# Decoder trunk: the MLP's weight sums go from VectorE to GpSimd, and the last group's squares, residual tiles and square sums are handed to other engines

## The reference, cut to what matters

```python
x = x + mixer_out(attn, rec, lp)              # MLA heads + RG-LRU
x = x + mem_attend(rmsnorm(x, norm_mem_g), mem_k, mem_v, lp)
h = rmsnorm(x, norm_mlp_g)
x = x + jnp.square(jax.nn.relu(h @ w_up)) @ w_down     # w_up 1024x4096, w_down 4096x1024
y = rmsnorm(x, final_norm_g)
```

## Time and profile before

| | before |
|---|---|
| median of 3 runs | 1017.05 us (1015.78 to 1017.05) |
| the profiled execution | 1017.48 us, its span 1015.3 us |
| PE busy | 973.6 us, 96% of the span |
| VectorE, GpSimd, ScalarE busy | 675.1, 430.2, 383.1 us |
| granted TensorE clock, mean | 0.989 |
| chain that ended last | PE 74%, VectorE 14%, ScalarE 4%, GpSimd 3% |

### The profile page before, as it was taken

The page is one execution under the profiler, slowest core; times in us unless marked ns, Lnnn a source line. Parts: engine busy times, 40 slices in busy tenths (PEclk is TensorE's granted clock), DMA queues, the critical chain, the costliest instruction groups (busy, mean ns, idle before and its releaser), DMA issues.

```text
span 1015.3 us, 20122 instructions
## 1 busy us (share of the span) xinstructions
PE 973.6 (96%) x8319; PEld 876.8 (86%) x8319; DVE 675.1 (66%) x1051; ACT 383.1 (38%) x774; POOL 430.2 (42%) x284
## 2 busy tenths in 40 slices
PE   6999999999999999999999999889999999999987
PEld 6989898766677777999975799889999999999986
DVE  5789978378655555564155366779577856957686
ACT  7334265465444443121045222334234333424344
POOL 4545579601011112555320155845375466628340
PEclk8999999999999999999999999999999999999999
DMA  8323355524277772832193036223340514144012
GB/s 235 81 67 83 104 158 141 152 95 186 116 277 272 282 279 69 280 96 85 30 398 138 1 90 180 64 83 93 95 125 23 166 43 125 43 125 114 12 42 88
DMA packets 140560, 130.41 MB, mean 128 GB/s; under 512 B 13477, under 2 KB 133170, under 8 KB 136630
## 3 DMA queue, kind: packets, MB, share of 16 engines
q1 hardware_dynamic: 134888, 88.55, 29.0%
q0 software_dynamic: 2304, 37.75, 9.6%
q10 hardware_dynamic: 3278, 2.83, 0.8%
HBM read 123.53 MB, written 5.03 MB: 127 GB/s over the span
## 4 chain that ended last, share of the span: by engine, by line
PE 74%; DVE 14%; ACT 4%; issue 3%; POOL 3%; DMA 2%; SPq 0%; DVEq 0%; ACTq 0%; POOLq 0%
PE gps L655 33%; PE gps L1286 7%; PE aux L1286 7%; PE gps L1015 5%; PE aux L1029 3%; PE aux L1056 3%; PE gps L791 2%; PE gps L1171 1%; PE gps L1253 1%; PE aux L1035 1%; POOL wlo L580 1%; PE gps L1091 1%; DVE pw_lo L2350 1%; PE aux L967 1%; DVE act_lo L1887 1%
## 5 line engine op out<-in xcount | busy, mean ns | idle before, releaser
L556 POOL TENSOR_SCALAR whi<-wraw 128x1024 fp32r<-128x1024 f32 (+1 forms) x77 | 83.4, 1083 | 291.1 <-PE gps L655 224.9
L655 PE MATMUL gps<-h_hi,whi 128*128 128x272 f32 x640 | 185.7, 290 | 2.6 <-POOL wlo L559 2.6
L655 PE MATMUL gps<-h_hi,wlo 128*128 128x272 f32 x640 | 185.5, 290 | 0.0
L655 PE MATMUL gps<-h_lo,whi 128*128 128x272 f32 x640 | 185.0, 289 | 0.0
L559 POOL TENSOR_TENSOR wlo<-wraw,whi 128x1024 fp32r<-128x1024 f32 (+1 forms) x77 | 178.9, 2323 | 6.4
L655 PE MATMUL gps<-act_hi,whi 128*128 128x272 f32 x448 | 132.5, 296 | 4.8 <-DVE act_lo L1887 4.1
L655 PE MATMUL gps<-act_lo,whi 128*128 128x272 f32 x448 | 130.9, 292 | 0.0
L655 PE MATMUL gps<-act_hi,wlo 128*128 128x272 f32 x448 | 130.4, 291 | 0.0
L592 POOL TENSOR_TENSOR pw_lo<-praw,pw_hi 128x512 fp32r<-128x512 f32 x64 | 94.9, 1491 | 77.7 <-ACT pw_hi L1772 76.9
L655 PEld LDWEIGHTS gps<-h_hi,whi 128*128 128x128 f32 x640 | 120.9, 189 | 3.4 <-POOL wlo L559 3.0
L655 PEld LDWEIGHTS gps<-h_lo,whi 128*128 128x128 f32 x640 | 120.7, 189 | 0.0
(11 more groups left out here) (431 smaller groups left out, 2371.4 us busy)
## 6 DMA issues: line engine op xcount, KB each, us to landing
wraw<-in_w_up_dram SPq DMA_DIRECT2D x32, 512.0 KB, 4.2
praw<-in_w_down_dram SPq DMA_DIRECT2D x32, 512.0 KB, 4.9
wraw<-in_w_in_dram SPq DMA_DIRECT2D x14, 512.0 KB, 4.1
kv<-in_cache_mem_k_dram SPq DMA_DIRECT2D x7, 1024.0 KB, 6.9
kv<-in_cache_mem_v_dram SPq DMA_DIRECT2D x7, 1024.0 KB, 14.0
wraw<-in_w_mem_k_dram SPq DMA_DIRECT2D x16, 256.0 KB, 3.1
wraw<-in_w_mem_v_dram SPq DMA_DIRECT2D x16, 256.0 KB, 3.3
wraw<-in_w_out_dram SPq DMA_DIRECT2D x8, 512.0 KB, 4.9
```

Of the source, the lines that this page charges most:

```text
L556: nc.gpsimd.tensor_scalar(whi[:, slot, 0:n], wraw[:, slot, 0:n], 1.0, 1.0, ALU.mult, ALU.mult).then_inc(pool_step, 1)
L655: mm = nc.tensor.matmul(out_of(a), w_of(w, k), x_of(x, k, part), start=(k == 0 and s == 0), stop=(k == k_tiles - 1 and s == 2))
```

## The change

All sixteen pairs' four sums move from VectorE to GpSimd. GpSimd's work for a pair in the down part is now eight operations in this order: sum 0, sum 1, low 0, low 2, sum 2, low 3, sum 3, low 5. Sum 0 of pair q waits, as before, until all of VectorE's low parts of the pairs before are made (`pair_lo_d`, 3q), since `s_sum` has one buffer.

In the up part GpSimd does the same for pair 4g behind the splits of tiles 2 to 6, and VectorE's low parts 1 and 4 of pair 4g stand behind tiles 2 and 4. Low part 6 of pair 4g is no longer in the up part: `down_pair` now begins with `pair_low(q, 6)` for the first pair of a group too, where it did so only `if p`.

In the last group GpSimd adds up the squares of tiles 1 to 5 (`gather_last`), ScalarE does the high part and the square of two tiles between the casts 2, 3 and 4 of a pair (`final_high`), and PE sums `acc` inside product 6 of the last pair and the squares of tiles 6 and 7 apart, into bank 3 of `gps`.

```diff
 POOL, up part and behind it
-                    for i in {2: (0,), 3: (2, 3), 5: (5,)}[j] if j in (2, 3, 5) else ():
-                        pair_low(4 * g, i)
+                    if j == 2:
+                        pair_sum_of(4 * g, 0)
+                        pair_sum_of(4 * g, 1)
...
                     if (g and j == 1) or (g == GROUPS - 1 and j == 7):
                         for q in range(4 * (g - (j == 1)) + 1, 4 * (g - (j == 1)) + 4):
-                            for i in POOL_LOW:
-                                pair_low(q, i)
+                            pair_sum_of(q, 0)
+                            pair_sum_of(q, 1)
+                            pair_low(q, 0)
+                            pair_low(q, 2)
+                            pair_sum_of(q, 2)
+                            pair_low(q, 3)
+                            pair_sum_of(q, 3)
+                            if q > 13:
+                                gather_last(2 * (q - 14))
+                            pair_low(q, 5)
+                            if q > 13:
+                                gather_last(2 * (q - 14) + 1)
 DVE, down part
-                if p:
-                    pair_low(q, 6)
+                pair_low(q, 6)
                 dve.wait_ge(pair_ps, 7 * q + 2)
                 V.tensor_tensor(x22, x22, c, ALU.subtract).then_inc(pair_ev, 1)
-                if ahead:
-                    pair_sums(q + 1, 0)
-                    pair_sums(q + 1, 1)
...
-                if last and p:
-                    gather_square(3, 2 * p - 2)
-                    gather_square(3, 2 * p - 1)
-                if ahead:
-                    pair_sums(q + 1, 2)
 DVE, up part
-                    if j == 0:
-                        pair_sums(4 * g, 0)
-                        pair_sums(4 * g, 1)
-                    if j == 1:
+                    if j == 2:
                         pair_low(4 * g, 1)
-                        pair_sums(4 * g, 2)
-                    if j == 2:
-                        pair_sums(4 * g, 3)
+                    if j == 4:
                         pair_low(4 * g, 4)
-                    if j == 3:
-                        pair_low(4 * g, 6)
 PE, product 6 of the last pair
+                    if (q, i, k) == (15, 6, 1):
+                        pe.wait_ge(pair_ev, 7 * 15)
+                        pe.wait_ge(nx_acc, 19)
+                        token_sums(acc[:, :], True)
```

More of the change, by code:

```diff
@@ L339, in low_ready @@
             return pair_lo_d, 3 * q + DVE_LOW.index(i) + 1
-        Y_BANKS = (((aux, 0), (aux, 1)), ((gps, 2), (aux, 2)), ((gps, 0), (gps, 3)), ((gps, 1), (aux, 0)),
+        Y_BANKS = (((aux, 0), (aux, 1)), ((gps, 2), (aux, 2)), ((gps, 0), (aux, 3)), ((gps, 1), (aux, 0)),
                    ((gps, 2), (aux, 1)))
@@ L593, in pair_low, with pair_sum_of, gather_last @@
                                         ).then_inc(pair_lo_p, 1)
+            def pair_sum_of(q, n):
+                raw = praw[q % 2]
+                if n == 0:
+                    pool.wait_ge(pair_raw[q % 2], REST_0 + 32 * (q // 2 + 1))
+                    if q:
+                        pool.wait_ge(pair_lo_d, 3 * q)
+                    nc.gpsimd.tensor_tensor(s_sum[:, :], raw[:, 1, 0, :], raw[:, 1, 1, :], ALU.add
+                                            ).then_inc(pair_sum, 1)
+                elif n == 1:
+                    pool.wait_ge(pair_sum, 4 * q + 1)
+                    nc.gpsimd.tensor_tensor(raw[:, 1, 0, :], raw[:, 0, 0, :], raw[:, 1, 0, :], ALU.add
+                                            ).then_inc(pair_sum, 1)
+                elif n == 2:
+                    pool.wait_ge(pair_sum, 4 * q + 2)
+                    pool.wait_ge(pair_lo_p, HALF_0 + 4 * q + 1)
+                    nc.gpsimd.tensor_tensor(raw[:, 0, 0, :], s_sum[:, :], raw[:, 0, 0, :], ALU.add
+                                            ).then_inc(pair_sum, 1)
+                else:
+                    pool.wait_ge(pair_sum, 4 * q + 3)
+                    pool.wait_ge(pair_lo_p, HALF_0 + 4 * q + 3)
+                    nc.gpsimd.tensor_tensor(raw[:, 0, 1, :], raw[:, 0, 0, :], raw[:, 0, 1, :], ALU.add
+                                            ).then_inc(pair_sum, 1)
+            def gather_last(k):
+                if k < 1:
+                    return
+                pool.wait_ge(nx_sq, 5 + 16 + k + 1)
+                if k >= 2:
+                    pool.wait_ge(nx_acc, 14 + k - 1)
+                nc.gpsimd.tensor_tensor(acc[:, :], acc[:, :], sqb[1][:, k % 2, :], ALU.add).then_inc(nx_acc, 1)
             for u in range(U_MLP + 8 * GROUPS):
@@ L630, in _ @@
                     g, j = divmod(u - U_MLP, 8)
-                    for i in {2: (0,), 3: (2, 3), 5: (5,)}[j] if j in (2, 3, 5) else ():
-                        pair_low(4 * g, i)
+                    if j == 2:
+                        pair_sum_of(4 * g, 0)
+                        pair_sum_of(4 * g, 1)
+                    if j == 3:
+                        pair_low(4 * g, 0)
+                        pair_low(4 * g, 2)
+                    if j == 4:
+                        pair_sum_of(4 * g, 2)
+                        pair_low(4 * g, 3)
+                    if j == 5:
+                        pair_sum_of(4 * g, 3)
+                    if j == 6:
+                        pair_low(4 * g, 5)
                     if (g and j == 1) or (g == GROUPS - 1 and j == 7):
                         for q in range(4 * (g - (j == 1)) + 1, 4 * (g - (j == 1)) + 4):
-                            for i in POOL_LOW:
-                                pair_low(q, i)
+                            pair_sum_of(q, 0)
[10 more added lines that the diff above has]
+                                gather_last(2 * (q - 14) + 1)
+                    if g == GROUPS - 1 and j == 7:
+                        gather_last(4)
+                        gather_last(5)
                 if u == U_OUT + 3:
@@ L1264, in moving, with token_sums @@
                         4: r[:, k, 0:HALF], 5: r[:, k, 2 * HALF:3 * HALF], 6: x[:, 4 + k, high]}[i]
+            def token_sums(squares, start):
+                for i in range(5):
+                    n = 128 if i < 4 else TS
+                    mm = nc.tensor.matmul(gps[0:n, 3, i:i + 1], squares[:, 128 * i:128 * i + n], ones[:, 0:1],
+                                          start=(start and i == 0), stop=True, skip_group_check=True)
+                return mm
             def pair_part(q, i, ks):
@@ L1343, in _ @@
             pe.wait_ge(pair_ev, 7 * 15 + 5)
-            for i, z in Y_ORDER[:3]:
+            for i, z in Y_ORDER[:2]:
                 y_turn(i, z)
[L1346 to L1350, removed]
-            pe.wait_ge(nx_sq, 5 + 8 * 3)
[L1352 to L1356, removed]
+            pe.wait_ge(nx_sq, 5 + 8 * 3 - 1)
+            token_sums(sqb[1][:, 0, :], False)
+            pe.wait_ge(nx_sq, 5 + 8 * 3)
+            token_sums(sqb[1][:, 1, :], False).then_inc(nx_ps, 1)
             pe.wait_ge(pair_ev, 7 * 16)
-            for i, z in Y_ORDER[3:]:
+            for i, z in Y_ORDER[2:]:
                 y_turn(i, z)
@@ L1814, in final_high @@
                 act.wait_ge(res_ok, 16 + k + 1)
-                if k < KD - 1:
-                    raw_hi(XG[:, k, :], k, "final_norm_g")
+                raw_hi(XG[:, k, :], k, "final_norm_g")
                 square_of(3, k)
-                if k == KD - 1:
-                    raw_hi(XG[:, k, :], k, "final_norm_g")
-            HIGH_AFTER = {0: (0, 1, 2, 3), 2: (4, 5, 6)}
+            HIGH_AFTER = {1: (0, 1, 2, 3), 3: (4, 5), 5: (6,)}
             for g in range(GROUPS):
@@ L1833, in _ @@
                         pair_copy(pair)
-                    if p < PAIRS - 1:
-                        for i in (0, 1, 2):
+                    for i in range(7):
+                        if p < PAIRS - 1:
                             pair_high(pair + 1, i)
[L1837 to L1844, removed]
+                        if g == GROUPS - 1 and p and i in (2, 4):
+                            final_high(2 * p - 2 + (i == 4))
+            for k in (6, 7):
+                act.wait_ge(res_ok, 16 + k + 1)
+                square_of(3, k)
+            for k in (6, 7):
+                raw_hi(XG[:, k, :], k, "final_norm_g")
             act.wait_ge(nx_var, 7)
@@ L2326, in _ @@
             raw_norm(2, T_MO, "norm_mlp_g")
[L2327 to L2345, removed]
             def pair_low(q, i):
@@ L2418, in down_pair @@
                 V.tensor_tensor(x12, b, x12, ALU.add).then_inc(pair_ev, 1)
-                if ahead:
-                    pair_sums(q + 1, 3)
                 dve.wait_ge(pair_ps, 7 * q + 6)
@@ L2437, in _ @@
                     up_tile(8 * g + j)
-                    if j == 0:
-                        pair_sums(4 * g, 0)
-                        pair_sums(4 * g, 1)
-                    if j == 1:
+                    if j == 2:
                         pair_low(4 * g, 1)
-                        pair_sums(4 * g, 2)
-                    if j == 2:
```

(9 more changed lines are left out.)

## The result

The changed kernel takes 1067.91 us (median of 4 runs, 1067.58 to 1068.95) against 1017.05 (4 runs, 1015.78 to 1019.18) for the kernel before: a ratio of 1.050, 95% interval 1.048 to 1.052. Its profiled execution has a span of 1065.8 us, 50.5 longer, and a mean granted clock of 0.969. The prediction was +49.7.

What follows compares the result with a forecast made beforehand. PE was taken to set the pace, so only 14.9 us could be won; losses of 56.1 (groups 0 to 2), 6.6 (group 3) and 1.9 (up part), less 14.9, gave +49.7: 1067.2 us, range 1055.5 to 1081.

Steps and rivals of the forecast that it cites:

- Part 2: Second pair of groups 0 to 2: late low part 6 delays SP's loads, so PE waits 14.3 us in each.
- Part 1: Down part: GpSimd's eight operations take 11.75 us a pair against PE's 10.55, so PE must wait 1.2 a pair.
- The two meetings of a pair: GpSimd operations beside two of VectorE's three low parts in a pair: 0.44 us extra each.
- rival C: GpSimd, all pairs: nearly every operation meets VectorE and pays 0.44 us, 31 more in all, 1098 us; chance 10%.
- The rule of the Trainium skill: GpSimd and two-input VectorE operations lock shared SBUF ports: up to 0.68 us an encounter, some 5 us over 12 pairs.
- The waits at product 3: Down pairs: PE waits for `p1s` at product 3, 2.0 us in the first pair behind a hold, 1.2 in each following.
- the cover: Products 0 to 2 after a hold: slower matmuls eat into product 3's 2.0 us wait, costing nothing; uncovered, 5 us.
- Group 3: Last group, no holds: waits at product 3 of 2.0, 1.2, 2.0, plus 0.3 and 1.1 in pair 15; 6.6 us together.
- The 14.9 us won: Whole MLP and behind it: 13.1 us of PE's waits and 1.8 of slow clock all go.
- split weights in group 0: First up part: GpSimd's splits and pair operations, 6.1 us against PE's 6.05, have no lead; 1.9 us lost.
- A: Rival: the next group's two tile loads come in time, only the pair rate remains, 1024.3 us; chance 5%.
- B: Rival, not slower: VectorE's low part 6 is done early, loads leave as before, 1015.4 us; chance 3%.

Runs made afterwards that it cites:

- the kernel with the loads first: Changed kernel, but SP issues the next group's two tile loads ahead of pair 4g+2's loads: 1028.9 us, ratio 1.011.
- the kernel without holds: Changed kernel with SP's loads of the next group's tiles issued first and low part 6 of pair 4g made one tile earlier: 1018.39 us, ratio 1.0018.

## Why the prediction held, step by step

- **Part 2, the holds (3 x 14.3 forecast).** Measured 13.8, 14.1 and 14.0: the place, the number of groups and each link of the chain are as forecast. Putting the loads first removes it, and the earlier low part 6 shortens it by its own shift; the move alone makes it in the kernel before.
- **Part 1, the pace (11.75 us a pair forecast).** GpSimd's sum 0 of two pairs that follow each other in group 2 starts at 913.24 and 924.86, 11.6 apart; a pair later, in group 0, it is 11.76 (706.39 and 718.15). On PE, product 3 of the last two pairs comes 11.76 to 11.79 apart in groups 0 to 2. Sum 0 to the end of low part 0 was to take 4.3 us and took 4.4. The operations by themselves, in the columns of the earlier trace rows:

```profile
L592 POOL TENSOR_TENSOR pw_lo<-praw,pw_hi x64: 1262/1292/2057, 643.7 to 1044.0; 128x512 fp32r<-128x512 f32 x64
...
L2388 DVE TENSOR_TENSOR pw_lo<-praw,pw_hi x32: 677/1106/1773, 661.9 to 1043.4; 128x512 fp32r<-128x512 f32 x32
...
L606 POOL TENSOR_TENSOR praw<-praw x16: 1266/1290/1300, 634.4 to 1034.3; 128x512 f32<-128x512 f32 x16
...
L616 POOL TENSOR_TENSOR praw<-praw x16: 1286/1548/1567, 656.3 to 1041.2; 128x512 f32<-128x512 f32 x16
```

  An add on GpSimd costs the 1.29 that was taken from a low part, and the median low part fell from 1.488 to 1.292, since VectorE's sums were what it met (1.492 again in the kernel whose sums went back to VectorE). The two meetings of a pair, taken at 0.44 each, cost 0.45 (low part 0, 1.72 to 1.76 us in the second to fourth pair of a group) and 0.26 (sum 3, the last line). The dear GpSimd of rival C would have needed 1.7. The rule of the Trainium skill that the prediction worked out beside Part 1 ("SBUF — State Buffer", the section "SBUF: two separate sides") was taken there at up to 0.68 an encounter, a pair up to 0.5 longer. The pairs show none of that; the last section has what the rule gives when it is read with the order in which the two begin.
- **The waits at product 3 (18.4 us forecast, 8.5 measured).** The size is off and the sum is not. Where nothing covers them, in the kernel with the loads first, they are 15.0: the list counts from the end of the product before, and product 3 comes 1.84 and 1.15 us late there where 2.0 and 1.2 were forecast (the prediction's own S + 10.95 less S + 8.85 is 2.1). The other 6.5 us are the cover. After each hold PE's granted clock is 0.50, the 1.2 GHz level; here the one in group 1:

```profile
805.00:809.00 4.00, 0.56 (x2) 0.59 (x3) 3.01 (x6) 1.75 (x3) 3.92 (x4) 0.50 0.00 0
809.00:813.00 4.00, 4.00 (x20) 4.00 (x19) 1.95 (x4) 1.14 (x2) 3.86 (x4) 0.50 0.00 0
```

  PE is slow where it would otherwise have waited for `p1s`, and GpSimd's pace sets the end of the group either way. What had been taken from the 3.7 us wait, 1.8 us, was too small for a hold of 14: in groups 1 and 2 products 0 to 2 took 7.3 us instead of 4.5, and the loss of 2.8 also ate the wait of the pair that followed. The cover, 2.0 + 1.2 + 1.2 = 4.4 a group in the forecast, held: from the start of the pair behind the hold to product 3 of the group's last pair it is 29.90, 29.91 and 29.90 us in the three groups, and 29.9 in the kernel with the loads first, where no clock was lost there.
- **Group 3.** Product 3 waits 1.64, 0.97 and 1.64 in the three pairs (2.0, 1.2, 2.0 forecast), 0.17 for low part 0 of pair 15 (0.3) and 1.23 for `acc` (1.1).
- **The 14.9 us won.** The waits of the earlier trace rows for VectorE and those put down to issue are gone, and those for `p1s` are counted anew above; 1.5 for split weights in group 0 remains (1.9 forecast, a figure that the prediction does not work out).
- **How near.** That forecast and result lie 0.7 us apart is in part luck: the terms alone come out 1.1 us too high in the MLP, and 1.8 us came from a later start of the MLP, which is in no term.
- **Rivals.** A was put at 1024.3 and the kernel made as A describes took 1028.9; B at 1015.4 and that kernel took 1018.4.

## What to carry to other kernels

SP's queue kept its order: the loads of the next group's tiles left 6.15 us behind the first product instead of 14 ahead of it, because the step before them waited. So before an operation is moved later, look for the transfer that waits for it, and then for all that stands behind that transfer in its queue, even for another stage. Work moved to an engine with idle time is judged by that engine's time for one round against the round of the engine that sets the pace, with the waits between them (11.75 against 10.55 us here at 48% busy), not by busy shares. A wait can cost nothing while a longer one covers it, and returns when that one is mended, so mend in the order of the chain and price each step again.

## What had not been expected of the hardware

**A whole operation of GpSimd can stand in VectorE's way, and whether it does differs from one profiled kernel to the next.** In the kernel before, a low part on VectorE in group 0 took 2.88 us instead of 0.68. It began 0.12 behind a split of GpSimd and ended 0.54 after it (VectorE's row first, then GpSimd's):

```profile
657.37 2.88 DVE L2350 TENSOR_TENSOR pw_lo<-praw,pw_hi 128x512 fp32r<-128x512 f32 x1
...
657.25 2.46 POOL L559 TENSOR_TENSOR wlo<-wraw,whi 128x1024 fp32r<-128x1024 f32 x1
```

It is one of two such rows in that group, and from there VectorE runs late until PE waits 3.7 us for it. In the kernel with the last group's changes alone, with the same order in group 0, that operation met a shorter one of GpSimd, took 1.78, and the 3.7 us wait isn't there:

```profile
658.44 1.78 DVE L2369 TENSOR_TENSOR pw_lo<-praw,pw_hi 128x512 fp32r<-128x512 f32 x1
...
658.17 1.50 POOL L592 TENSOR_TENSOR pw_lo<-praw,pw_hi 128x512 fp32r<-128x512 f32 x1
```

So a part of what was counted as won (3.7 and the 1.8 of clock behind it) hangs, it seems, on how the two engines happen to meet, and not on the change; no run isolates it. GpSimd lost less in such meetings: 0.1 to 0.5 us before, 0.77 at most in the changed kernel. Four rows of the changed kernel show that it goes by the same measure on both sides:

```profile
658.69 2.40 POOL L559 TENSOR_TENSOR wlo<-wraw,whi 128x1024 fp32r<-128x1024 f32 x1
...
660.51 1.45 DVE L2420 TENSOR_TENSOR rx_lo<-rx,rx_hi 128x816 fp32r<-128x816 f32 x1 [0.31 <-ACT rx_hi L1872]
...
661.05 2.06 POOL L592 TENSOR_TENSOR pw_lo<-praw,pw_hi 128x512 fp32r<-128x512 f32 x1
...
661.89 1.77 DVE L2388 TENSOR_TENSOR pw_lo<-praw,pw_hi 128x512 fp32r<-128x512 f32 x1
```

By themselves the last three take 1.01, 1.29 and 0.68 us. Each begins while the row above it still runs, and each ends its own time, less some 0.14 us, behind that row's end: 661.09 + 1.01 - 0.14 = 661.96, then 661.96 + 1.29 - 0.14 = 663.11, then 663.11 + 0.68 - 0.14 = 663.65 (measured 663.66). This holds all through the MLP of both kernels. Each of the 42 GpSimd operations of 128x512 in the changed kernel (48 before) that begin while a VectorE operation with two inputs in SBUF runs loses what VectorE still had to run, less 0.12 to 0.16; those that begin first or alone take 1.26 to 1.32 in the changed kernel. A VectorE operation of 128x512 that comes second ends 0.55 behind GpSimd's, and one that comes first takes its own 0.68. This agrees with the rule of the Trainium skill that the prediction names, a port held for a whole operation, from both sides: who begins second pays, and how much is what the first has left. VectorE met long operations of GpSimd, so it lost more.

**The tail's clock.** From the first sum over `acc`, in product 6 of the last pair, the same instructions took 15.6 us in the changed kernel (1050.19 to its end at 1065.8) and 19.6 in the kernel without holds (997.36 to 1017.0). PE waited 1.2 us for `acc` ahead of it in both; in the first the clock stayed at its full level, 2.4 GHz, for over 6 us, in the second it fell to 1.2 GHz some 2 us behind the first sum (here the windows that begin 1.8 and 2.6 us behind it, in the changed kernel and then in the kernel without holds):

```profile
1052.00:1054.00 2.00, 2.00 (x20) 2.00 (x19) 0.44 (x1) 0.72 (x2) 0.00 (x0) 1.00 0.00 0
```

```profile
1000.00:1002.00 2.00, 2.00 (x12) 2.00 (x10) 0.44 (x1) 1.29 (x3) 0.00 (x0) 0.50 0.00 0
```

Among the profiles of six kernels with that wait (one each) it fell within 2 us in three; in the other three, and in the two kernels without the wait, it fell 5.8 us or more behind the first sum. That the wait lets it fall is thus possible, and not shown. Together with a start of the MLP that moves by up to 6.6 us between profiles, this may be why single runs of the later kernels spread over 2 to 13 us; differences of 2 us between them stay open.
